# Two blocks of a transformer on one core: the order of VectorE's rests and ScalarE's output copies in the attentions

## The reference, cut to what matters

```python
# first block, layer 0: 8 heads, 96 wide, values 64 wide, causal
scores = einsum("bqhd,bkhd->bhqk", q_blk, k) * 96 ** -0.5
probs = softmax(where(k_idx <= q_idx, scores, -inf)); out = einsum("bhqk,bkhd->bqhd", probs, v)
# first block, layers 0 and 1: 4 heads, 128 wide, 512 queries on 256 keys of a memory, no mask
probs = softmax(einsum("bqhd,bmhd->bhqm", q, k) * 128 ** -0.5); out = einsum("bhqm,bmhd->bqhd", probs, v)
# second block, both layers: 8 heads, 64 wide, that share one key and one value head and see the
# top 256 keys by a score of their own, and 8 heads with their own keys and a forget term
logits = einsum("bqhd,bshd->bhqs", qb, k) * 64 ** -0.5 + cum_q - cum_k; p = softmax(where(causal, logits, -1e30))
```

## Time and profile before

| | us |
|---|---|
| median of 3 runs | 3485.95 |
| lowest, highest | 3484.33, 3487.09 |
| the profiled execution, its own time | 3481.1 |
| its span, first to last instruction | 3479.4 |

### The profile page before, as it was taken

The page is one execution under the profiler, slowest core; times in us unless marked ns, Lnnn a source line. Parts: engine busy times, 40 slices in busy tenths (PEclk is TensorE's granted clock), DMA queues, the critical chain, the costliest instruction groups (busy, mean ns, idle before and its releaser), DMA issues. The chain is left out here.

```text
span 3479.4 us, 49589 instructions
## 1 busy us (share of the span) xinstructions
PE 3382.2 (97%) x19379; PEld 2816.2 (81%) x19379; DVE 1797.5 (52%) x3311; ACT 1474.9 (42%) x2970; POOL 1431.9 (41%) x1268
## 2 busy tenths in 40 slices
PE   8999999999999999999999998999999999999999
PEld 7878778888877787888888778888888877888887
DVE  4655574636466574565353376445153285445243
ACT  4662354323344454532333347344343246444343
POOL 3220154455443445444544431345554441245543
PEclk9999999999999999999999999999999999999999
DMA  4210024545221122344533220222322220132321
GB/s 120 73 43 15 26 85 137 190 145 188 81 97 37 37 85 97 109 150 154 174 132 117 83 73 1 73 85 91 103 82 100 95 73 25 38 96 97 96 92 55
DMA packets 232837, 317.89 MB, mean 91 GB/s; under 512 B 9910, under 2 KB 149149, under 8 KB 232605
## 3 DMA queue, kind: packets, MB, share of 16 engines
q1 hardware_dynamic: 203206, 261.55, 23.3%
q10 hardware_dynamic: 29398, 53.17, 4.5%
HBM read 312.59 MB, written 2.10 MB: 90 GB/s over the span
## 5 line engine op out<-in xcount | busy, mean ns | idle before, releaser
L364 PE MATMUL banks<-split,split 128*128 128x512 f32 (+2 forms) x11760 | 2678.0, 389 | 16.7 <-ACT split L383 7.0
L364 PEld LDWEIGHTS banks<-split,split 128*128 128x128 f32 x11760 | 2183.4, 188 | 487.8 <-ACT split L383 15.6
L387 POOL TENSOR_TENSOR split<-kept,split 128x512 fp32r<-128x512 f32 (+2 forms) x1158 | 1355.9, 1175 | 1719.2 <-ACT split L383 1716.5
L383 ACT ACTIVATE split<-kept 128x512 fp32r<-128x512 f32 (+2 forms) x1158 | 646.2, 564 | 1463.8 <-PE banks L364 1418.2
L1590 DVE SCALAR_TENSOR_TENSOR work<-banks,kept,work 128x511 f32<-128x511 f32 (+1 forms) x176 | 120.4, 746 | 257.1 <-ACT work L1572 256.3
L910 DVE SCALAR_TENSOR_TENSOR work<-work,kept 128x512 f32<-128x512 f32 x168 | 194.5, 1157 | 6.0
L855 DVE SCALAR_TENSOR_TENSOR kept<-banks,kept 128x512 f32<-128x512 f32 x48 | 33.3, 745 | 209.6 <-PE banks L364 209.6
L853 DVE TENSOR_TENSOR kept<-banks,kept 128x512 f32<-128x512 f32 x64 | 40.6, 684 | 195.0 <-PE banks L364 195.0
L540 DVE COPY work<-banks 128x512 f32<-128x512 f32 (+1 forms) x64 | 37.4, 644 | 195.4 <-PE banks L364 195.3
L1165 PE MATMUL banks<-work 128*128 128x128 f32 x928 | 136.4, 277 | 0.3
L1165 PEld LDWEIGHTS banks<-work 128*128 128x128 f32 x928 | 118.6, 192 | 4.9 <-ACT work L1241 1.9
(11 more groups left out here) (410 smaller groups left out, 3117.3 us busy)
## 6 DMA issues: line engine op xcount, KB each, us to landing
work<-in_mod_w ACTq DMA_DIRECT2D x48, 1024.0 KB, 6.4
kept<-in_ffn_w SPq DMA_DIRECT2D x94, 512.0 KB, 4.8
kept<-in_w_up SPq DMA_DIRECT2D x88, 512.0 KB, 4.5
kept<-in_w_in SPq DMA_DIRECT2D x36, 1024.0 KB, 5.0
kept<-in_od_w_in SPq DMA_DIRECT2D x20, 1024.0 KB, 5.1
kept<-in_ffn_w SPq DMA_DIRECT2D x18, 1024.0 KB, 5.2
kept<-in_w_down SPq DMA_DIRECT2D x18, 1024.0 KB, 5.0
kept<-in_ev_w_in SPq DMA_DIRECT2D x8, 1024.0 KB, 5.1
```

Of the source, the lines that this page charges most:

```text
L364: m = pe.matmul(self.bank(q, j), lhs, rhs, start=t == 0 and i == 0, stop=t == job.KT - 1 and i == 2)
L383: act.activation(self.weights(s, 0), self.source(s), ACT.Copy).then_inc(self.rounded, 1)
L387: pool.tensor_tensor(self.weights(s, 1), self.source(s), self.weights(s, 0), ALU.subtract).then_inc(self.k.slices_split, 1)
```

## The change

In each attention VectorE's loop runs `out` last in its step, behind the rests of the next head's query and keys and behind `rest_o`; before, `out` came first. ScalarE's loop runs `round_o` in the step in which TensorE turns the output, behind `take_p`; before, in the step after. No instruction is added or removed, and TensorE, GpSimd and SyncE keep their order.

```diff
@@ go_on_scalar
             self.take_p(act, u)
-            if self.turned_o(u - 1) is not None:
-                self.round_o(act, self.turned_o(u - 1))
+            if self.turned_o(u) is not None:
+                self.round_o(act, self.turned_o(u))
@@ go_on_vector
             if u + 2 < self.units:
                 self.peak(dve, u + 2)
-            if u >= 1:
-                self.out(dve, link, u - 1)
+            if self.turned_o(u - 1) is not None:
+                self.rest_o(dve, self.turned_o(u - 1))
             if t == 0 and h + 1 < H:
                 self.rest_q(dve, h + 1)
                 if self.new_keys(h + 1):
                     self.rest_k(dve, h + 1)
-            if self.turned_o(u - 1) is not None:
-                self.rest_o(dve, self.turned_o(u - 1))
+            if u >= 1:
+                self.out(dve, link, u - 1)
```

## The result

| | before | after |
|---|---|---|
| median of 4 runs each, us | 3486.3 | 3455.3 |
| lowest and highest | 3484.33 to 3487.09 | 3455.05 to 3455.43 |
| profiled execution, us (span) | 3481.1 (3479.4) | 3455.43 (3453.7) |

The ratio of the medians is 0.9912, with a 95% interval from 0.9897 to 0.9926: 31.0 us faster, inside the forecast range and 1.8 us under the forecast. The two profiled executions are only 25.7 us apart, 5.3 less.

What follows compares the result with a forecast made beforehand. It took TensorE, 97% busy, as the bound, idling on handshakes with VectorE and ScalarE. 12.9 us per sixteen-head attention, 25.8 for two, plus 2.2 and 0.9, made 28.9, taking the median from 3485.95 to 3457.1 us, range 3453 to 3463.

Steps and rivals of the forecast that it cites:

- own keys, unturned: Heads with their own keys and no turn_o in their third step: 1.56 us less each, 6.2 per sixteen-head attention.
- the bank stall: TensorE's turn of keys waits for rest_o to free its bank; the whole 1.08 us goes.
- part 1: rest_q and rest_k ahead of out on VectorE; an unturned head with its own keys gains 0.48 us.
- part 2: rest_o ahead of out and round_o a step earlier, belonging together; the keys' bank stall of 1.08 us goes whole.
- own keys, turned: Heads with own keys and turn_o in their third step: 0.78 us each, 3.1 per attention, turn_o covering the late exponential.
- shared keys, unturned: Heads 1, 3, 5: the loop through mix, exponential and turn_p loses rest_q, 0.69 us each, 2.1 per attention.
- shared keys, turned: Heads 2 and 6: the whole score stall goes, turn_o as cover, 0.39 us each, 0.8 per attention.
- head 4: The one head with the forget rows on VectorE as well: put at 0.7 us.
- each cross attention: Only the place of out counted at the keys' turn, 0.45 us each, between 0 and 1.1.
- The reserve on ScalarE: Time to spare at turn_p and its mix after the early round_o delays exponential and take_p: some 0.6 to 0.8 us.
- (b): Rival: every wait vanishes, the exponential of t=3 being no bound; some 34 us in all, 3452; chance 0.12.
- (c): Rival: no change, since work on engines at 52% and 42% beside one at 97% is free; 3486 us; chance 0.05.

Runs made afterwards that it cites:

- part 2 alone: Kernel before, with only round_o a step earlier and rest_o ahead of out; query and key rests stay behind out: 3473.8 us, ratio 0.9972.
- part 1 alone: Kernel before, with only rest_q and rest_k ahead of out; rest_o stays behind out, round_o a step late: 3468.88 us, ratio 0.9955.
- e3_late_copy: Changed kernel with round_o put back a step later on ScalarE, VectorE's new order kept: 3469.45 us, ratio 0.9959.
- e4_rest_o_last: Changed kernel with rest_o put back behind out on VectorE, round_o staying early: 3465.09 us, ratio 0.9946.
- e8_twelve_extra: Changed kernel with twelve unused one-column ScalarE copies behind each early round_o in the attentions of sixteen heads: 3464.0 us, ratio 0.9937.
- e5_query_first: Changed kernel with rest_q also ahead of the peak of its step where the next head has own keys: 3452.57 us, ratio 0.9908.

## Why the prediction was right, step by step

The forecast was 3457.1 us; the runs gave 3455.3. The layer comes out closer than its terms do, and that is luck: own keys turned came in 0.2 us lower, shared keys turned 0.3 higher. By its own steps:

| step | forecast | measured |
|---|---|---|
| own keys, unturned (7, 9, 11, 13) | 1.56 each, 6.2 | 1.55 to 1.57, 6.3 |
| of it: the bank stall | 1.08 | 1.04 (part 2 alone) |
| of it: part 1 | 0.48 | 0.54 (part 1 alone), 0.53 (both less part 2) |
| own keys, turned (8, 10, 12, 14) | 0.78 each, 3.1 | 0.70 to 0.73, 2.9 |
| shared keys, unturned (1, 3, 5) | 0.69 each, 2.1 | 0.66 to 0.67, 2.0 |
| shared keys, turned (2, 6) | 0.39 each, 0.8 | 0.54 each, 1.1 |
| head 4 | 0.7 | 0.66 |
| layer | 12.9 | 12.86 |
| first attention | 2.2 | 2.13 |
| each cross attention | 0.45 | 0.98 |
| wait of turn_p, t=3, own keys (0 before) | about 0.3 | 0.19 |
| the same, shared keys (0.50 before) | 0.20 | 0.30 |

**Right, and shown.** The bound of the unturned head is the reading on which most hung: 0.48 instead of the 0.79 that TensorE alone would allow. In after turn_p waits there for the exponential, so it is the chain and not TensorE that ends last, but by 0.19 and not by 0.31. The unturned heads gain 0.54 from part 1 where the turned ones, without that wait, gain 0.72. The peak of t=3 (3.91 forecast, 3.90 measured) and turn_p (5.49, 5.48) were right in place; TensorE's own bound was not, as the next paragraph shows. That round_o and rest_o belong together, e3_late_copy and e4_rest_o_last show. The reserve on ScalarE was put at "some 0.6 to 0.8" at turn_p and its mix; e8_twelve_extra gives 0.93 with own keys, and there take_q runs out first, which I had not priced. At heads 3 and 5, where I had worked out none, the reserve is 0.20 and 0.09, the narrowest place in the sixteen heads. "rest_q right behind the peak" and "no 0.44 before `out`" stand in the rows above.

**Turned heads with own keys: 0.78, measured 0.70 to 0.73.** I had turn_o cover all of the exponential's lateness, and it does. Head 12 in before, then in after:

```profile
2170.23 0.19 PEld L1426 LDWEIGHTS banks<-split,split 128*128 128x128 f32 x1 [0.89 <-DVE split L1461]
```

```profile
2159.73 0.19 PEld L1426 LDWEIGHTS banks<-split,split 128*128 128x128 f32 x1 [0.17 <-issue]
...
2161.61 0.46 PEld L1153 LDWEIGHTS banks<-kept,work 128*128 128x128 f32 x4
```

turn_p of t=3 loads 0.13 behind the last load of the scores ahead of it (2161.48), without a wait, as it did before. What was too large is the 0.79 itself. The scores load 4.53 after turn_q before (2165.70) and 3.80 in after (2155.93): 0.73, which is the head's gain. I had them at 3.68, with rest_q at 2.20 after turn_q; it starts at 2.31. What is left is the scores' wait for rest_k, 0.17 in the row and 0.26 by the distance of the loads, and that is what e5_query_first took away. So what I expected of that experiment was too low at both kinds of head (0.12 and 0.3, measured 0.24 and 0.45): I had counted the chain and not the sooner scores.

**Turned heads with shared keys: 0.39, measured 0.54.** I gave them the scores' stall alone. They are unchanged with part 2 alone, and have the 0.54 with part 1 alone, so it is part 1. The term stopped at the wait that the rows showed. The profile of before has two things beyond that in head 2, whose turn_q loads at 2095.41:

```profile
2098.58 0.19 PEld L1426 LDWEIGHTS banks<-split,split 128*128 128x128 f32 x1 [0.38 <-DVE split L1461]
...
2100.36 0.42 PEld L1153 LDWEIGHTS banks<-kept,work 128*128 128x128 f32 x4
```

The scores come 3.17 after turn_q, in after 2.71: 0.46 sooner, though the wait says 0.38. And turn_p of t=3 comes 0.26 behind the last load of the scores ahead of it (2100.10), in after 0.14; it loads 0.87 after its exponential starts (2099.49), the same distance as in the unturned heads. So turn_o did not cover the exponential here, and the sooner peak gave 0.12 more, in a place where the profile names no wait.

**Cross attentions: 0.45 each, measured 0.98.** The term of the sum that was furthest off, with two causes. The stall of L1129 went from 1.10 to 0.57:

```profile
515.29 0.68 DVE L1310 TENSOR_TENSOR split<-banks,split 128x512 fp32r<-128x512 f32 x1
...
515.89 0.34 DVE L1304 TENSOR_SCALAR work<-banks,work 128x128 f32<-128x128 f32 x1
```

That is 0.54, near my 0.45. The other 0.45 (net of the 0.27 that the early copy costs there) is the step that I counted as nothing, "the remaining moved copies have no turn of keys behind them". True of the keys; but at the end of a cross attention the last turn of the output (L1172) waits for the last `out`, and in the kernel before a rest_o was queued directly ahead of that one, behind the `out` before it. In after it stands ahead of both and is through 0.44 us before the last one starts, from 0.18. VectorE before, then after:

```profile
526.56 0.69 DVE L1310 TENSOR_TENSOR split<-banks,split 128x512 fp32r<-128x512 f32 x1
...
527.43 0.35 DVE L1304 TENSOR_SCALAR work<-banks,work 128x128 f32<-128x128 f32 x1
```

```profile
525.82 0.69 DVE L1310 TENSOR_TENSOR split<-banks,split 128x512 fp32r<-128x512 f32 x1 [0.64 <-ACT split L1245]
...
526.95 0.35 DVE L1304 TENSOR_SCALAR work<-banks,work 128x128 f32<-128x128 f32 x1
```

and TensorE's wait there went from 1.22 to this:

```profile
527.35 0.42 PEld L1172 LDWEIGHTS banks<-kept,work 128*128 128x128 f32 x4 [0.72 <-DVE work L1304]
```

My bounds for the remaining copies were -0.3 to +0.1. They should have been drawn from the nearest wait, 1.22 us at that turn, and not from the absence of a turn of keys.

**The rivals.** (b), every wait vanishes, gave 3452. The time falls between it and the forecast, but its mechanism did not happen: L1153's wait for L1233 is there, 8.0 us in 27 times, 0.19 of it in each of the heads where (b) would have none. (c), no change, fell by 31 us. It carried the rule that the Trainium skill gives in Perfetto Trace Analysis, under Identifying the Most-Contended Engine, that an improvement comes in general from the engine with the highest occupancy. TensorE was busiest with 97%, its instructions were left alone, and reordering engines at 52% and 42% gave 0.9%. This does not refute the rule, for it was TensorE's idle time that shrank: in the first attention of sixteen heads from 12% to 2%. It refutes what I made of it in (c), that the time stays when TensorE's own instructions do.

**One step of the sum was loose.** The five attentions gave 29.8 us, 0.9 over the forecast: the cross attentions 1.1 over, the rest 0.2 under. I subtracted from the profiled execution and added its distance to the median, 4.85. That held: 29.8 us out of 3486.3 would be 3456.5, and the runs gave 3455.3, a difference well inside the interval of the ratio. The profiled pair alone would have shown 25.7.

## What to carry to other kernels

An engine that runs its instructions in order makes every instruction behind a wait pay for that wait: look at the first idle gap on the helper engine, ask which queued instructions do not need what it waits for, and put the one that the busiest engine needs next ahead of it. Then price the move by the second-latest chain, not by the stall removed; here TensorE alone would have allowed 0.73 us in such a head and 0.54 arrived, and the other 0.19 came only when that second chain was shortened too. A producer and its consumer on two engines may have to move together: here one of them alone gave nothing and the other a quarter.

## What the runs showed of the hardware

**Losses that belong to the execution.** after_again is the changed kernel once more. The same windows in before, in after and in after_again (columns as in the first windows above; the granted clock is the third number from the end):

```profile
2050.00:2100.00 50.00, 47.59 (x270) 40.12 (x269) 30.62 (x102) 24.45 (x62) 14.05 (x20) 1.00 0.19 63
```

```profile
2050.00:2100.00 50.00, 48.15 (x272) 40.85 (x272) 29.02 (x103) 25.72 (x66) 13.49 (x19) 0.97 0.16 53
```

```profile
2050.00:2100.00 50.00, 48.15 (x293) 41.49 (x292) 30.71 (x107) 28.30 (x74) 13.29 (x19) 1.00 0.13 43
```

With the clock at 1.00 the stretch ahead of the sixteen heads takes 636.54 us in after_again, as in before (636.53); at 0.97 in after, 638.12. The 1.6 us come and go with the same program. So do the others: the first L1117 load comes at 150.77 in before, 152.22 in after and 150.86 in after_again, and the third turn_q, from which the first attention is counted, at 162.13, 164.61 and 162.21; the granted clock of 150 to 200 is 0.97, 0.93 and 0.97. e5_query_first shows the same 0.97 in 2050 to 2100 and in 2850 to 2900, which may be why its median gives less than its stretches. What lowers the clock, no run here tells. The practical side: of two single executions of this kernel the difference is uncertain by some 3 to 5 us, while one head's turn_q to turn_q repeats within 0.01 to 0.02.

**Small copies.** Two copies of one column on ScalarE are shown as 0.29 us together but hold the next instruction for 0.19, and twelve, shown as 1.22, for 1.12: 0.093 to 0.095 each.
